# A hybrid attention and pooling step on one core: where the later modulations are summed

## What is computed

```python
mod = silu(c) @ w_ada + b_ada              # one for context (c_ctx), one for latent tokens (c)
sh1, sc1, g1, sh2, sc2, g2 = split(mod, 6) # six vectors of 2048
h = layer_norm(x) * (1 + sc1) + sh1
m = mixer(h)                               # w_in, gated linear attention in two directions, pooling, w_out
x = layer_norm(ALPHA * x + g1 * m)
h = x * (1 + sc2) + sh2
f = (silu(gate) * up) @ w_down             # gate, up = split(h @ w_gu)
x = layer_norm(ALPHA * x + g2 * f)
```

## Time and profile before

| | us |
|---|---|
| median of 3 runs | 2781.84 |
| lowest and highest | 2778.35, 2788.09 |
| span of the profiled execution, first to last instruction | 2776.4 |

### The profile page before, as it was taken

One profiled execution on the slowest core, in us unless ns is written; L12 is line 12 of the kernel. 1 busy time (PEld: TensorE's weight loads), 2 busy tenths in 40 slices (PEclk: granted clock), 3 DMA queues, 4 the chain that ended last, 5 costly groups with the idle time before them and its releaser, 6 DMA issues.

```text
span 2776.4 us, 37655 instructions
## 1 busy us (share of the span) xinstructions
PE 2681.7 (97%) x16224; PEld 2401.2 (86%) x16224; DVE 1404.1 (51%) x1598; ACT 904.8 (33%) x939; POOL 650.8 (23%) x216
## 2 busy tenths in 40 slices
PE   5999999999998999999999999999999999999997
PEld 3678788788986878999999999999999888888875
DVE  4322222325566457656555545555556444445578
ACT  4332323332212125433333333333333323333243
POOL 0000000000000000244434444344443333333440
PEclk9999999999999999999999999999999999999999
DMA  9765546552356233223333223332234746454576
GB/s 376 278 231 197 196 168 211 199 181 72 104 184 206 95 121 105 92 92 106 106 106 102 85 96 106 106 106 90 92 101 144 250 179 215 171 208 163 197 240 237
DMA packets 179385, 438.13 MB, mean 158 GB/s; under 512 B 9980, under 2 KB 25732, under 8 KB 173076
## 3 DMA queue, kind: packets, MB, share of 16 engines
q1 hardware_dynamic: 176916, 430.48, 45.2%
q10 hardware_dynamic: 2304, 5.24, 0.5%
HBM read 401.83 MB, written 33.85 MB: 157 GB/s over the span
## 4 chain that ended last, share of the span: by engine, by line
PE 75%; DVE 8%; DMA 7%; POOL 3%; ACT 2%; issue 2%; SPq 1%; ACTq 0%; POOLq 0%; DVEq 0%
PE ps L2191 10%; PE ps L2192 10%; PE ps L2193 10%; PE ps L2268 6%; PE ps L2270 6%; PE ps L2269 6%; PE ps L1944 5%; PE ps L1946 5%; PE ps L1945 5%; PE ps L1985 4%; PE ps L1924 3%; PE ps L2138 2%; PE ps L2140 2%; PE ps L2139 2%; DMA raw_w<-w_gu_b 2%
## 5 line engine op out<-in xcount | busy, mean ns | idle before, releaser
L1579 DVE TENSOR_TENSOR w_lo<-raw_w,w_hi 128x1024 fp32r<-128x1024 f32 x264 | 334.4, 1268 | 297.9 <-ACT w_hi L1151 295.1
L1151 ACT ACTIVATE w_hi<-raw_w 128x1024 fp32r<-128x1024 f32 x264 | 270.1, 1054 | 598.8 <-POOL raw_w L888 347.7
L2191 PE MATMUL ps<-x_hi,w_hi 128*128 128x320 f32 x1408 | 435.7, 309 | 2.1 <-DVE x_lo L1659 1.4
L2193 PE MATMUL ps<-x_hi,w_lo 128*128 128x320 f32 x1408 | 435.1, 309 | 0.0
L2192 PE MATMUL ps<-x_lo,w_hi 128*128 128x320 f32 x1408 | 435.1, 309 | 0.0
L1714 DVE TENSOR_TENSOR x_lo<-low,x_hi 128x2560 fp32r<-128x2560 f32 (+2 forms) x55 | 221.1, 4023 | 260.3 <-ACT x_hi L1244 260.3
L879 POOL TENSOR_TENSOR low<-raw_w 128x1024 f32<-128x1024 f32 x41 | 102.7, 2505 | 1065.0 <-DMA raw_w<-w_gu_b 1052.0
L2268 PE MATMUL ps<-w_hi,x_hi 128*128 128x512 f32 x880 | 343.1, 390 | 5.7 <-DVE x_lo L1714 2.4
L2269 PE MATMUL ps<-w_lo,x_hi 128*128 128x512 f32 x880 | 342.4, 389 | 0.0
L2270 PE MATMUL ps<-w_hi,x_lo 128*128 128x512 f32 x880 | 342.3, 389 | 0.0
L2191 PE MATMUL ps<-low_r,w_hi 128*128 128x320 f32 x1072 | 332.1, 310 | 2.2 <-DVE w_lo L1579 1.5
(11 more groups left out here) (222 smaller groups left out, 4342.3 us busy)
## 6 DMA issues: line engine op xcount, KB each, us to landing
raw_w<-w_gu_b SPq DMA_DIRECT2D x180, 512.0 KB, 5.7
low<-w_ada SPq DMA_DIRECT2D x68, 1024.0 KB, 5.3
raw_w<-w_down SPq DMA_DIRECT2D x55, 1024.0 KB, 5.2
low<-hidden_scratch SPq DMA_DIRECT2D x33, 1280.0 KB, 6.1
raw_w<-w_in_b SPq DMA_DIRECT2D x33, 1024.0 KB, 8.0
x_raw<-w_ada SPq DMA_DIRECT2D x25, 1024.0 KB, 15.3
raw_w<-w_out SPq DMA_DIRECT2D x16, 1024.0 KB, 5.1
hidden_scratch<-high SPq DMA_DIRECT2D x44, 320.0 KB, 5.9
```

The lines of the kernel that those rows point to most:

```text
L1151: nc.scalar.activation(weight(0, w), src, ACT.Copy).then_inc(prod_hi, 1)
L1579: nc.vector.tensor_tensor(weight(1, n), src, weight(0, n).bitcast(F32), ALU.subtract).then_inc(prod_split, 1)
L2191: mm(out, wh, version(v, 0, k), start=first and k == 0, stop=False)
L2193: ins = mm(out, wl, version(v, 0, k), start=False, stop=last and k == HK - 1)
```

## The change

For the 16 later sums TensorE no longer multiplies the blocks. `w_ada` comes in 256 pieces of 128 rows by 512 columns (256 KB, 2 KB a row), into a ring of five slots of 512 columns. For each piece, 16 to a sum:

- ScalarE scales it by the context's conditioning value of each partition into one of three temporary slots (Copy with a scale), and GpSimd adds that to an accumulator (or copies it, for the first piece).
- VectorE multiplies the same piece by the latent tokens' conditioning value and adds it to another accumulator in one `scalar_tensor_tensor` (or `tensor_scalar`, for the first).

When 16 pieces are in, TensorE folds the 128 partitions of the two accumulators with indicator columns of ones: "adasum" has two products of 512 columns, "adacol" eight of 2. These items stand six quarters after the last piece, and the row store seven. "adarow" is gone. The load of piece i+4 is issued at item i, once ScalarE and VectorE are both done with piece i−1. A sum's accumulators are used again two sums later: both engines then wait for the fold, and GpSimd for the row store too. ScalarE waits for GpSimd to be done with piece i−3. Bank 3 becomes "C": the third part of "outer" and the folds use it.

```diff
-RING = 2
+ADA_ACC = (640, 1152, 1664)
+ADA_TMP = 3
+RING = 5
+RING_LAG = 1
-ADA_STEPS = 4 * N_ADA
+ADA_PARTS = 16
+ADA_STEPS = ADA_PARTS * N_ADA
...
     for i in range(ADA_STEPS):
         at = ADA_FROM + i * (ADA_TO - ADA_FROM) // ADA_STEPS
-        put(0, at, ("ada", i // 4, i % 4))
-        if i % 4 == 3:
-            put(0, at, ("adarow", i // 4, 0))
-            if ADA[i // 16][1] == "col":
-                put(0, at + 1, ("adacol", i // 4, 0))
+        a, m = divmod(i, ADA_PARTS)
+        put(0, at, ("ada", a, m))
+        if m == ADA_PARTS - 1:
+            if ADA[a // 4][1] == "col":
+                put(0, at + 6, ("adacol", a, 0))
             else:
-                put(0, at + 1, ("adasum", i // 4, 0))
-                put(0, at + 2, ("row_store", i // 4, 0))
+                put(0, at + 6, ("adasum", a, 0))
+                put(0, at + 7, ("row_store", a, 0))
...
-    need = {"gate": "A", "cum": "B", "score": "AB", "outer": "ABA", "mix": "AB", "norm": "A",
-            "vT": "B", "poolmm": "AB", "adasum": "B", "adacol": "A"}
+    need = {"gate": "A", "cum": "B", "score": "AB", "outer": "ABC", "mix": "AB", "norm": "A",
+            "vT": "B", "poolmm": "AB", "adasum": "C", "adacol": "C"}
...
         def load_ada(i):
-            a = i // 4
+            a, m = divmod(i, ADA_PARTS)
             if i >= RING:
-                sp.wait_ge(ada_used, i - RING + 1)
+                sp.wait_ge(ada_act, i - RING + 1)
+                sp.wait_ge(ada_vec, i - RING + 1)
             else:
                 sp.wait_ge(unit_used, EARLY)
-            sp.dma_start(ring_slot(i), w_ada_v[ADA[a // 4][0], a % 4, i % 4]).then_inc(ada_in[i % RING], 16)
+            sp.dma_start(ring_slot(i), w_ada_h[ADA[a // 4][0], a % 4, m]).then_inc(ada_in[i % RING], 16)
...
             elif kind == "ada":
-                i = 4 * a + b
-                if i + RING < ADA_STEPS:
-                    load_ada(i + RING)
+                i = ADA_PARTS * a + b + RING - RING_LAG
+                if RING <= i < ADA_STEPS:
+                    load_ada(i)
...
-        pool.wait_ge(ada_used, ADA_STEPS)
+        for i in range(ADA_STEPS):
+            a, m = divmod(i, ADA_PARTS)
+            acc, src = acc_pool(a), scaled_slot(i)
+            if m == 0 and a >= 2:
+                x, k = sum_of(a - 2)
+                pool.wait_ge(filled[x], k + 1)
+                if ADA[(a - 2) // 4][1] == "row":
+                    pool.wait_ge(row_out, 16 * rows_before(a - 1))
+            pool.wait_ge(ada_act, i + 1)
+            if i:
+                pool.wait_ge(ada_pool, i)
+            else:
+                pool.wait_ge(ones_row, 1)
+            if m == 0:
+                nc.gpsimd.tensor_copy(acc, src).then_inc(ada_pool, 1)
+            else:
+                nc.gpsimd.tensor_tensor(acc, acc, src, ALU.add).then_inc(ada_pool, 1)
+        pool.wait_ge(ada_pool, ADA_STEPS)
+        pool.wait_ge(ada_vec, ADA_STEPS)
...
+            elif kind == "ada":
+                i = ADA_PARTS * a + b
+                act.wait_ge(ada_in[i % RING], 16 * (i // RING + 1))
+                if i >= ADA_TMP:
+                    act.wait_ge(ada_pool, i - ADA_TMP + 1)
+                nc.scalar.activation(scaled_slot(i), ring_slot(i), ACT.Copy, scale=cond_of(b, 0)).then_inc(ada_act, 1)
...
+            elif kind == "ada":
+                i = ADA_PARTS * a + b
+                acc, src = acc_vec(a), ring_slot(i)
+                if b == 0 and a >= 2:
+                    x, k = sum_of(a - 2)
+                    dve.wait_ge(filled[x], k + 1)
+                dve.wait_ge(ada_in[i % RING], 16 * (i // RING + 1))
+                if b == 0:
+                    nc.vector.tensor_scalar(acc, src, cond_of(0, 1), None, ALU.mult).then_inc(ada_vec, 1)
+                else:
+                    dve.wait_ge(ada_vec, i)
+                    nc.vector.scalar_tensor_tensor(acc, src, cond_of(b, 1), acc, ALU.mult,
+                                                   ALU.add).then_inc(ada_vec, 1)
...
-            elif kind == "ada":
-                i = 4 * a + b
-                if i == 0:
-                    pe.wait_ge(zin_evac, 2)
-                elif b == 0:
-                    pe.wait_ge(ada_row, a)
-                pe.wait_ge(ada_in[i % RING], 16 * (i // RING + 1))
-                ada_step(3, ring_slot(i), b, ada_used)
...
             elif kind == "adasum":
                 x, k = uses[0]
-                pe.wait_ge(ada_row, a + 1)
+                pe.wait_ge(ada_pool, ADA_PARTS * (a + 1))
+                pe.wait_ge(ada_vec, ADA_PARTS * (a + 1))
                 take(x, k)
-                mm(pair(x, 512)[0:2, :], group_sum, high[:, H_ROW:H_ROW + 512],
-                   start=True, stop=True).then_inc(filled[x], 1)
+                for c, acc in enumerate((acc_pool(a), acc_vec(a))):
+                    ins = mm(pair(x, 512)[0:2, :], indicator(c), acc, start=c == 0, stop=c == 1)
+                ins.then_inc(filled[x], 1)
```

More of the change, by code:

```diff
@@ L304, in backbone @@
     w_ada_v = w_ada.rearrange("(m k p) (g q c) -> g q m p k c", p=P, k=4, g=6, q=4)
+    w_ada_h = w_ada.rearrange("(k p) (g q c) -> g q k p c", p=P, g=6, q=4)
     w_out_v = w_out.rearrange("(kg k p) (nb c) -> nb kg p k c", kg=4, k=4, p=P, nb=4)
@@ L382, in ring_slot, with scaled_slot, cond_of, acc_pool @@
     def ring_slot(i):
-        return lo(L_PA + (i % RING) * STEP, STEP).rearrange("p (k c) -> p k c", k=4)
+        return lo(L_PA + 512 * (i % RING), 512)
+    def scaled_slot(i):
+        return lo(L_PA + 512 * (RING + i % ADA_TMP), 512)
+    def cond_of(k, c):
+        return cols(C_CS + 2 * k + c, 1)
+    def acc_pool(a):
+        return high[:, ADA_ACC[a % 2]:ADA_ACC[a % 2] + 512]
+    def acc_vec(a):
+        return cols(C_COND, 512) if a % 2 else high[:, ADA_ACC[2]:ADA_ACC[2] + 512]
     FIRST_USES = [[i for i in range(FIRST_STEPS) if FIRST_SLOT[i] == n] for n in range(N_FIRST)]
@@ L511, in backbone @@
     ada_in = [sem(f"ada_in{i}") for i in range(RING)]
[L512 to L513 removed]
+    ada_act = sem("ada_act")
+    ada_pool = sem("ada_pool")
+    ada_vec = sem("ada_vec")
     row_out = sem("row_out")
@@ L594, in scan_index, with sum_of, rows_before @@
         return 2 * h + d
+    def sum_of(a):
+        key = ("adasum" if ADA[a // 4][1] == "row" else "adacol", a, 0)
+        return USES[key][0]
+    def rows_before(a):
+        return sum(1 for i in range(a) if ADA[i // 4][1] == "row")
     def gate_row(nb, i):
@@ L742, in _ @@
                     sp.wait_ge(spilled[x], 16 * n_out[x])
+                for x in range(3):
                     sp.wait_ge(drained[x], FILLS[x])
@@ L917, in _ @@
         act.wait_ge(cond_zero, 1)
+        nc.scalar.activation(cols(C_CS, 2 * KT), vec(V_COND, 32), ACT.Silu)
         nc.scalar.activation(cond_pad[:, :, 0:2], vec(V_COND, 32).rearrange("p (k c) -> p k c", c=2),
@@ L1114, in _ @@
                 act.wait_ge(filled[x], k + 1)
-                nc.scalar.activation(high[0:2, H_ROW:H_ROW + 512], pair(x, 512)[0:2, :],
+                nc.scalar.activation(acc_pool(a)[0:2, :], pair(x, 512)[0:2, :],
                                      ACT.Copy).then_inc(drained[x], 1)
@@ L1990, in take @@
                 pe.wait_ge(drained[x], k)
-            elif x == 0:
-                pe.wait_ge(zin_evac, EARLY)
+            elif x != 1:
+                pe.wait_ge(zin_evac, EARLY if x == 0 else 2)
         for kind, a, b, uses in SCHEDULE:
@@ L2101, in _ @@
                 x, k = uses[0]
[L2102 removed]
+                pe.wait_ge(ada_pool, ADA_PARTS * (a + 1))
+                pe.wait_ge(ada_vec, ADA_PARTS * (a + 1))
                 take(x, k)
[L2104 to L2105 removed]
+                for c, acc in enumerate((acc_pool(a), acc_vec(a))):
+                    ins = mm(pair(x, 512)[0:2, :], indicator(c), acc, start=c == 0, stop=c == 1)
+                ins.then_inc(filled[x], 1)
             elif kind == "adacol":
                 x, k = uses[0]
[L2108 removed]
+                pe.wait_ge(ada_pool, ADA_PARTS * (a + 1))
+                pe.wait_ge(ada_vec, ADA_PARTS * (a + 1))
                 take(x, k)
                 for kk in range(4):
[L2111 to L2112 removed]
+                    for c, acc in enumerate((acc_pool(a), acc_vec(a))):
+                        ins = mm(pair(x, 8)[:, 2 * kk:2 * kk + 2], acc[:, kk * P:(kk + 1) * P], indicator(c),
+                                 start=c == 0, stop=c == 1)
                 ins.then_inc(filled[x], 1)
         pe.wait_ge(zin_evac, N_IN)
[L2117 removed]
+        for x in range(3):
             pe.wait_ge(drained[x], FILLS[x])
```

21 lines of the change are left out of this document (13 added, 8 removed).

## The result

| | before | after |
|---|---|---|
| median of the runs, us | 2783.29 (4 runs) | 2900.59 (4 runs) |
| lowest and highest | 2778.35, 2788.09 | 2896.65, 2906.16 |
| span of the profiled execution | 2776.4 | 2902.6 |

The changed kernel is slower: ratio 1.0435, 95% interval 1.0416 to 1.0455. The medians of the table differ by 117 us (1.042). The forecast was 110 us more, and 2892.

What follows compares the result with a forecast made beforehand. TensorE was taken to bound the kernel before; afterwards VectorE with the path it shares with GpSimd: 179 + 458 − 57 − 10 = 570 us against 460, +110 on the 2781.84 median: 2892, range 2795 to 2965.

Steps and rivals of the forecast that it cites:

- The lock between VectorE and GpSimd: SBUF path: VectorE instructions with two SBUF inputs and GpSimd instructions reading SBUF exclude each other; the second waits.
- The sign: Whole kernel: slower 0.79, within 0.3% 0.05, faster 0.16; it turns on whether the lock holds for the new sums.
- The 70 us taken off TensorE: TensorE's queue in the stretch: 76.8 + 9 − 9 − 7, some 70 us less, to about 390.
- The open point: VectorE's new sums: no row showed scalar_tensor_tensor with two SBUF inputs against GpSimd; taken to behave as tensor_tensor.
- the shared step: One step's hold on the shared path: 0.61 us on VectorE and 1.18 on GpSimd, 1.79 where both queue.
- The sum: Stretch of the steps: VectorE's 179 us with stops, plus 458 for shared steps, less 57 overlap and 10: 570 us.
- my 48 adds: GpSimd adds counted as falling beside VectorE's PSUM work: 16 + 32, at 1.18 us each, 57 us off.
- The lower bound: Stretch of the steps with the shared path never idle: 504 us against 460, so +44.
- What was costed at nothing: 256 smaller loads on SyncE through the ring, and GpSimd's waits for row stores at six sums: 0 us.
- The one without the lock: Rival: no lock for these operations, so the kernel is some 45 to 50 us faster, 2735; chance 0.16.
- The turning point of 1.36 us a step: Shared step's cost at which the kernel would be neither slower nor faster, in place of 1.79.
- The ring as the bound: Rival: ring of loads sets the pace, four steps per 7.4 us load, 474 us, +14: 2796; chance 0.05.

Runs made afterwards that it cites:

- Experiment 2: Changed kernel with VectorE's sums accumulating in PSUM bank 3, only last pieces written to SBUF, outer product and folds back in pairs A and B: 2820.5 us, ratio 1.0156.
- experiment 3: Changed kernel with GpSimd's adds covering 256 of the 512 columns, VectorE's operations unchanged: 2814.6 us in one run.
- experiment 1: Changed kernel with GpSimd's 240 adds replaced by two fills each, which read nothing: 2781.5 us in one run.
- experiments 4, 5: Each from the changed kernel: 4 loads only the first five pieces and reuses them, 2884.0 us; 5 stores folded rows from their own place, 2885.0 us, ratio 1.0377.
- experiment 9: Kernel before, with 8 of 16 sums kept on TensorE, the others in pieces on VectorE, ScalarE and GpSimd, ring of two: 2893.3 us, ratio 1.0419.
- experiment 8: Filling-GpSimd kernel (experiment 1) plus rows of their own and four unit banks: 2788.3 us; then also loading only the first five pieces: 2763.9 us, one run each.

## Why the prediction was right, point by point

**The size and its cause.** The lock between VectorE and GpSimd makes most of the loss, as forecast. Experiment 2 takes one input of VectorE out of SBUF and gets 80 of the 117 us back; experiment 3 shortens GpSimd's instruction and VectorE's gets shorter. In the stretch, VectorE's sums are 34% of the chain that ended last.

**The sign.** The prediction let the sign hang on the lock: with it slower, without it some 47 us faster. That was not so. Without the lock on the sums the kernel takes 2820.5 us with GpSimd's adds (2803.6 with rows of their own) and 2781.5 with fills, so it is slower or the same there too. The 70 us taken off TensorE came through in no version that does the work, and this the prediction did not have.

**The open point.** Whether scalar_tensor_tensor behaves as tensor_tensor does in the earlier trace rows, is settled: it does. This is what the Trainium skill states for any DVE instruction with two SBUF inputs (SBUF — State Buffer, "Who interferes with whom"), and the trace agrees: 1.70 us a step for 0.75 and 1.26 alone. That nothing is lost where GpSimd only writes, experiment 1 shows.

**The prices.** VectorE's sum alone 0.75 taken, 0.75 measured at the least; GpSimd's add 1.31 taken, 1.26 measured; the shared step 1.79 taken, 1.70 measured; ScalarE's scaled copy 0.63 taken, 0.72 measured (its scale comes from a tile; whether that is the reason was not tried).

**The sum.** The forecast put the stretch at 570 us, it took 610, from 137 us on; against the true 470 of before that is 140 where 110 were said, and 11 came back behind it, where I had taken 10 off inside it. Its two halves were off in opposite ways. VectorE was busy 485 us: 127.6 of old work, some 15 us more for low parts and links that wait for the lock, and 344 for the sums, whose mean of 1.38 shows that more of GpSimd's work fell beside other work than my 48 adds. But VectorE also stood still for 125 us, where the prediction had 51: besides the 56 inside the links, it waited 27 us for TensorE's part of links and folds, 11 for loads and 7 for ScalarE's high parts, and the rest, some 24 us, is put down here to the spacing between dependent instructions, which the 1.79 had held. A queue that sets the pace still waits for its neighbours. That 2892 came within 9 us of 2900.6 is therefore in part luck: the late start of the window, the row stores and the ring were left out, the overlap with GpSimd was put too low, and these errors partly cancelled. The lower bound has a slip too: 19 × 2.15 and 24 × 0.71 are 58 us and not 65, so it is 497 us, or +37; the range's lower edge would have been 2794 in place of 2801.

**The path to TensorE.** The prediction had TensorE wait for the weights' low parts (L1318) and for VectorE's links. None of its waits is for a low part (L1374), and some 41 of the 146 us are for VectorE's instructions at all. The other 105 are for ScalarE's evacuations and copies. So the slow pair reached TensorE mostly through ScalarE's queue, whose scaled copies waited 115 us for GpSimd and 81 for loads, and whose links waited 69 for VectorE; the prediction had taken that queue as one that fits.

**What was costed at nothing.** The row stores cost 16 us and the ring 17 (experiments 4, 5). Neither was free (the ring's figure is from one run).

**The rivals.** The one without the lock was rightly put aside, but its price of 2735 was wrong by its own step, "not all 70 us come through: some 45 to 50". Experiment 1 gives 2781.5: none comes through, though loads and row stores, which the prediction costed at nothing, are in that time too. The turning point of 1.36 us a step was too high: with GpSimd's least of 0.72 in experiment 3 a step holds the path for some 1.2 us, and the kernel is still 36 us slower than before. The ring as the bound was wrong here; in experiment 9, with a ring of two, waits for loads are the largest of ScalarE and VectorE.

**What would have shown it wrong.** "TensorE's waits for the low parts (L1318) and for the chain's VectorE lines grow from about 15 us to some 170": all its waits together are 146, and most are others. "The granted clock may fall; that costs little": it fell to 0.84. Whether that costs anything in the changed kernel, or is hidden behind the other queues, no run shows; without lock and loads it is up to 25 us of the stretch by the estimate above. That it falls because of the waits was not tested; the rows show both in the same stretches and neither in the next.

## What to carry to other kernels

Before work is moved to GpSimd beside a busy VectorE, add up one path for both: every VectorE instruction with two SBUF inputs and every GpSimd instruction that reads SBUF. In experiment 2 an input in PSUM took VectorE out of that sum. And work that is taken off the bounding engine and put between the links of a chain, on queues that follow one schedule, must be charged its delays to the chain, its loads and its stores: here, without the lock (experiment 1), they ate all of 70 us, and in experiment 8, without loads and row stores too, still some 55.

## What the runs showed of the hardware that was not expected

TensorE's granted clock went from 0.99 to 0.84 in a stretch in which it waited 146 of 610 us, and to 0.93 in one in which it waited 43 of 466. The recorded mean of a main matmul hides this: 325 ns before, 345 and 326 there; the starts show it (0.27 us apart at 1.2 GHz, 0.15 at 2.4). How far the clock falls for so few stops was not expected; whether it follows the length or the number of the stops was not tried.
